# Three blocks in one program: first slabs k-tile by k-tile, the router in rounded parts, a norm factor applied later, and block 3's weights in rounded halves

## The reference, cut to what matters

```python
# block 1: rms_norm -> RWKV-7 heads and differential attention, each times a sigmoid gate, then an MLP
gates = jax.nn.sigmoid(p_gate).reshape(bsz, seqlen, N_BRANCH, D_MODEL)
merged = gates[:, :, 0] * o_rwkv + gates[:, :, 1] * o_diff
h_res = h_res + merged @ w_out[layer]
# block 2: layer_norm -> three linear-attention mixers -> branches -> ln1 -> 16 experts -> ln2
h = layer_norm(ALPHA * h + mix, ln1_g[l], ln1_b[l])
ffn = grouped_moe(h, w_router, router_bias, w_gate[l], w_up[l], w_down[l])
h = layer_norm(ALPHA * h + ffn, ln2_g[l], ln2_b[l])
# block 3: four attentions of four heads each on one projection, silu gates, one output projection
hn = rms_norm_3(x, norm_gain)
proj = jnp.einsum('btd,de->bte', hn, w_in)
...
return x + jnp.einsum('bte,ed->btd', y, w_out)
```

## Time and profile before

| what | us |
|---|---|
| median of 3 runs | 3912.48 (3900.85 to 3927.08) |
| the profiled execution's own time | 3914.93 |
| its span, first to last instruction | 3913.0 |
| PE busy | 3478.7 (89%) |
| weight loads busy | 2787.6 (71%) |
| DVE / ACT / POOL busy | 1604.3 / 1237.1 / 360.7 |
| mean granted clock of PE | 0.905 of full speed |

### The profile page before, as it was taken

The page is one execution under the profiler, slowest core; times in us unless marked ns, Lnnn a source line. Parts: engine busy times, 40 slices in busy tenths (PEclk is TensorE's granted clock), DMA queues, the critical chain, the costliest instruction groups (busy, mean ns, idle before and its releaser), DMA issues.

```text
span 3913.0 us, 69039 instructions
## 1 busy us (share of the span) xinstructions
PE 3478.7 (89%) x29806; PEld 2787.6 (71%) x29806; DVE 1604.3 (41%) x2836; ACT 1237.1 (32%) x2049; POOL 360.7 (9%) x337
## 2 busy tenths in 40 slices
PE   7888898889788999998788878879899999889998
PEld 6767777778668999996566666657578878355544
DVE  4443544454423343333445355566543344321222
ACT  3223322232322233233434455432222221232341
POOL 4121121112102100000011001110000000000000
PEclk9788897798859999999988889989899999988998
DMA  3001010011004233321112112123133333211111
GB/s 118 21 29 31 21 37 28 23 32 37 21 10 151 86 109 92 92 87 54 55 49 63 46 55 70 55 110 100 46 92 92 92 92 92 67 41 43 33 49 38
DMA packets 72448, 240.70 MB, mean 62 GB/s; under 512 B 8272, under 2 KB 8272, under 8 KB 70736
## 3 DMA queue, kind: packets, MB, share of 16 engines
q1 hardware_dynamic: 65088, 209.17, 17.8%
q0 software_dynamic: 3600, 20.83, 1.4%
q10 hardware_dynamic: 3456, 6.29, 0.4%
HBM read 221.44 MB, written 14.81 MB: 60 GB/s over the span
## 4 chain that ended last, share of the span: by engine, by line
PE 76%; DVE 11%; ACT 9%; issue 3%; DMA 1%; ACTq 0%; DVEq 0%; POOL 0%; SPq 0%; POOLq 0%
PE psum L410 74%; DVE arena L346 5%; ACT arena L331 5%; ACT arena L339 3%; DVE arena L355 2%; PE psum L414 1%; ACT L327 1%; DVE ring L346 1%; DVE arena L350 1%; ACT L331 1%; DMA ring<-in_w 1%; DVE arena L358 0%; DVE arena L367 0%; DVE arena L373 0%; DVE arena L370 0%
## 5 line engine op out<-in xcount | busy, mean ns | idle before, releaser
L410 PE MATMUL psum<-arena,ring 128*128 128x264 f32 (+2 forms) x6248 | 1576.7, 352 | 16.2 <-DVE arena L346 10.6
L410 PE MATMUL psum<-arena,arena 128*128 128x264 f32 (+2 forms) x6160 | 1498.4, 346 | 52.8 <-DVE ring L346 19.8
L410 PE MATMUL psum<-arena 32*32 32x32 f32 (+18 forms) x16376 | 1085.6, 248 | 319.8 <-ACT arena L331 82.4
L410 PEld LDWEIGHTS psum<-arena 32*32 32x32 f32 (+12 forms) x16376 | 771.2, 139 | 623.8 <-issue 277.6
L410 PEld LDWEIGHTS psum<-arena,arena 128*128 128x128 f32 (+1 forms) x6160 | 1013.2, 192 | 218.1 <-issue 52.9
L410 PEld LDWEIGHTS psum<-arena,ring 128*128 128x128 f32 (+1 forms) x6248 | 999.4, 197 | 208.3 <-issue 128.7
L339 ACT ACTIVATE arena<-psum 128x512 f32<-128x512 f32 (+12 forms) x625 | 282.8, 452 | 926.7 <-PE psum L410 817.6
L346 DVE TENSOR_TENSOR ring<-ring,arena 128x1024 fp32r<-128x1024 f32 (+1 forms) x297 | 354.3, 1193 | 515.2 <-ACT arena L339 511.2
L339 ACT ACTIVATE arena<-ring 128x1024 fp32r<-128x1024 f32 (+1 forms) x297 | 304.6, 1026 | 604.7 <-PE psum L410 552.3
L346 DVE TENSOR_TENSOR arena<-arena 128x528 f32<-128x528 f32 (+9 forms) x660 | 327.2, 496 | 245.3 <-ACT arena L331 130.4
L346 DVE TENSOR_TENSOR arena<-arena,psum 88x192 f32<-88x192 f32 (+5 forms) x428 | 193.5, 452 | 536.5 <-PE psum L410 526.2
(11 more groups left out here) (39 smaller groups left out, 840.3 us busy)
## 6 DMA issues: line engine op xcount, KB each, us to landing
ring<-in_w SPq DMA_DIRECT2D x313, 512.0 KB, 3.5
ring<-in_w SPq DMA_DIRECT2D x134, 256.0 KB, 2.6
bg<-arena ACTq DMA_DIRECT2D x24, 256.0 KB, 2.0
arena<-in_x SPq DMA_DIRECT2D x2, 2112.0 KB, 11.4
arena<-bg POOLq DMA_DIRECT2D x1, 3072.0 KB, 17.2
od<-arena POOLq DMA_DIRECT2D x8, 264.0 KB, 2.4
oy<-arena POOLq DMA_DIRECT2D x8, 264.0 KB, 2.4
arena<-oy POOLq DMA_DIRECT2D x2, 1056.0 KB, 7.8
```

The lines of the kernel that those rows point to most:

```text
L410: self.last_ins = self.eng.matmul(out, l, r, start=start, stop=stop, skip_group_check=skip)
```

## The change

- **Gates.** The gate products of k = 2 move to the heads' end, behind PE's `end` event, with their weight halves made by POOL before its oy transfer and their sigmoids on ACT ahead of the gates stage's first copies. Six buffers instead of four hold the gates. In block 1 ACT's root for kk comes one step earlier.
- **Mixers.** The first two slabs are computed together, k-tile by k-tile (`pe_two3`).
- **Branches.** The first four slabs (four high buffers instead of three) are split ahead of the waits for the mixers' ends. ln1's mean sum is spread over the last eight linears (`pe_add`), and the experts' first slabs are split before ln1.
- **Experts.** x's high part is made by ACT and the low part by DVE from the scaled value; slabs 0 and 1 follow k-tile by k-tile. The router comes behind them in three rounded products per k-tile with the router weights as the stationary side, is turned back by four transposes (`scores`), and DVE's router steps stand behind expert 0's products. The shares are turned behind slab 4. ln2's mean sum is spread as ln1's.
- **Block 3.** x's rounded parts times the gain are made without the norm's root; the sum of squares, the forget product and the first q product run together k by k. The root is multiplied in when DVE takes each product out of PSUM. All slabs come in halves that POOL splits, and all products are in rounded parts. v is computed like the others, then transposed. y is split for the last projection.

```diff
@@ -571,13 +571,19 @@
...
+    if run.highs >= len(run.offs) and run.then:
+        act_more(K, run.then)
+    else:
+        act_hi(K, run, run.highs)
+        run.highs += 1
...
@@ -594,6 +600,26 @@
...
+
+
+def pe_two3(K, first, second, xh, xl, of):
+
+    P, T, todo = K.P, xh[0].shape[1], []
+    for wh, wl, emptied, m in (first, second):
+        todo.append((wh, wl, K.ps[0:m, 512 * P.bank(1, *emptied):][:, 0:T], m))
+    for k in range(8):
+        P.wait_ge(*K.book.at(*of[k]))
+        for n, (wh, wl, out, m) in enumerate(todo):
+            P.mm3([out], wh(k)[:, 0:m], wl(k)[:, 0:m], xh[k], xl[k], k == 0, k == 7)
+            if k == 7:
+                yield n
+
+
+def pe_add(K, b, src, k, *of):
+
+    P, T = K.P, src.shape[1]
+    P.wait_ge(*K.book.at(*of))
+    P.mm(K.ps[:, 512 * b:512 * b + T], K.c["ones"], src, k == 0, k == 7)
...
@@ -1046,24 +1072,29 @@
...
+    for g in range(2):
+        gate(g, 2)
...
@@ -1088,7 +1119,7 @@
...
-                if nme == "v" and step == 1:
+                if nme == "v" and step == 0:
                     A.wait_ge(*at("rw_kk", hp))
                     A.inv_root(h2(m.dd[2]), out_of(K, 2, T, "rw_kkroot", hp), "rw_kkroot", hp, bias=K.c["tiny"])
...
@@ -1196,6 +1227,8 @@
...
     A.stage_end("act", "heads")
+    for g in range(2):
+        act_gate(K, m, g, 2)
...
@@ -1631,7 +1664,8 @@
...
-    assert m.wr.lows == len(m.wr.offs) or not K.book.known
+    while m.wr.lows < len(m.wr.offs):
+        pool_half(K, m.wr)
     G.wait_ge(*at("end", "pe", "heads"))
...
@@ -1957,7 +1991,8 @@
...
-               wh[0:3], [("slab", "mixers", 68)] * 3)
+               wh[1:4] + wh[0:1], [("slab", "mixers", 65 + i) for i in range(4)])
+    m.wx.then = m.wb
...
@@ -2053,13 +2089,10 @@
...
+    two = [pe_take(K, m.wx, w0)[1:] + (("gd_lr",), 40), pe_take(K, m.wx, w0 + SLAB)[1:] + (("gd_pad", 0, 0), 128)]
+    for i in pe_two3(K, *two, m.hh_r, m.h_r, [("normed", "ln0", k) for k in range(8)]):
+        P.did("slab", "mixers", i)
+        P.also(*(("gd_proj", 0, 0) if i else ("gd_lrp",)))
...
@@ -2839,34 +2876,44 @@
         pe_lin3(K, m.wb, i, ("b_y", i), m.Oh_r, m.O_r, [("b_Osplit", j) for j in range(12)], 4, 4 * (i % 3))
...
+        if k == 0:
+            b = K.P.bank(1, "centred", "ln1", 7)
+            K.P.keep(b)
+        else:
+            pe_add(K, b, m.h[:, (k - 1) * T2:k * T2], k - 1, "b_h", k - 1)
+    pe_add(K, b, m.h[:, 7 * T2:8 * T2], 7, "b_h", 7)
+    K.P.did("mean", "ln1")
+    K.P.drop(b)
...
     A, at, T = K.A, K.book.at, T2
+    act_first(K, m.wb)
     A.wait_ge(*at("end", "pe", "mixers"))
     A.wait_ge(*at("end", "dve", "mixers"))
     A.wait_ge(*at("end", "pool", "mixers"))
-    act_first(K, m.wb)
...
+    dve_first(K, m.wb)
+    split_dve(V, m.Oh_r[11][:], m.O[:, 11 * T:12 * T], m.O_r[11][:], "b_Osplit", 11)
     V.wait_ge(*at("end", "pe", "mixers"))
     V.wait_ge(*at("end", "act", "mixers"))
     V.wait_ge(*at("end", "pool", "mixers"))
-    dve_first(K, m.wb)
-    split_dve(V, m.Oh_r[11][:], m.O[:, 11 * T:12 * T], m.O_r[11][:], "b_Osplit", 11)
...
@@ -2891,9 +2938,12 @@
...
+        if k == 7:
+            dve_more(K, m.we)
+            dve_more(K, m.we)
...
@@ -2917,29 +2967,54 @@
...
+            P.mm3([ps[0:16, 512 * b:512 * b + 512]], m.wrh[:, R], m.wrl[:, R], m.xh_r[k], m.x_r[k], k == 0, k == 7)
...
+    def shares():
+        P.wait_ge(*at("r_w"))
+        b = P.bank(1, "r_ct")
+        for j in range(4):
+            P.tr(ps[0:16, 512 * b + 128 * j:512 * b + 128 * j + 128], m.R["w"][:, 16 * j:16 * j + 16])
+        P.did("r_tr")
+
+    two = [pe_weights(K, m.we, i) + (("e_up" if i else "e_silu", 0, 0), 128) for i in range(2)]
+    for i in pe_two3(K, *two, m.xh_r, m.x_r, [("e_xlow", j) for j in range(8)]):
+        P.did("slab", "experts", i)
+    router()
+    i = 2
...
-            for f in range(2):
...
+            for f in range(2) if e else (1,):
...
+                if e == 0:
+                    scores()
+                if e == 1 and f == 0:
+                    shares()
                 pe_lin3(K, m.we, i + 1, ("e_up", e, f), m.xh_r, m.x_r)
+                if e == 1 and f == 0:
+                    P.wait_ge(*at("r_ct"))
+                    share(0)
                 i += 2
-            if e == 0:
...
-                P.wait_ge(*at("r_ct"))
-            b = P.bank(1, "e_share", e)
-            P.mm(ps[:, 512 * b:512 * b + 512], s16[0:16, e, :], m.cT[0:16])
-            P.did("e_row", e)
+            if e:
+                share(e)
...
@@ -2950,19 +3025,25 @@
...
+    for k in range(8):
+        A.wait_ge(*at("ln1_g", k))
+        A.act(m.xh_r[k][:], m.x[:, k * T:k * T + T], ACT.Identity, "e_xhi", k, bias=K.p["ln1_b"][:, k:k + 1])
     A.wait_ge(*at("end", "pe", "branches"))
     A.wait_ge(*at("end", "dve", "branches"))
-    act_first(K, m.we)
...
@@ -2987,21 +3071,64 @@
...
+    dve_first(K, m.we)
+    V.wait_ge(*at("root", "ln1"))
+    for k in range(9):
+        if k < 8:
+            S = slice(k * T, k * T + T)
+            V.stt(m.x[:, S], m.h[:, S], p["ln1_g"][:, k:k + 1], m.rs, MUL, MUL, "ln1_g", k)
+        if k:
+            V.wait_ge(*at("e_xhi", k - 1))
+            V.stt(m.x_r[k - 1][:], m.x[:, (k - 1) * T:k * T], p["ln1_b"][:, k - 1:k], m.xh_r[k - 1][:], ADD, SUB, "e_xlow", k - 1)
     V.wait_ge(*at("end", "pe", "branches"))
     V.wait_ge(*at("end", "act", "branches"))
-    dve_first(K, m.we)
...
+            if e == 0:
+                dve_router(K, m, e3)
+                V.wait_ge(*at("r_tr"))
+                V.cp(m.cT[0:16], out_of(K, 1, T, "r_ct", m1=16), "r_ct")
+            V.wait_ge(*at("e_row", e))
+            for f in range(2):
+                kx = 2 * (e % 8) + f
+                S = slice(kx * T, (kx + 1) * T)
+                if e == 8 and f == 0:
+                    V.wait_ge(*at("slab", "experts", 47))
+                V.tt(m.Hl[:, S], m.esg[f], out_of(K, 1, T, "e_share", e), MUL, "e_sg", e, f)
+                if f:
+                    K.book.put(("e_share", e), K.book.now["e_sg", e, f])
+                split_dve(V, m.Hh_r[kx][:], m.Hl[:, S], m.Hl_r[kx][:], "e_H", half, kx)
...
@@ -3192,33 +3280,35 @@
...
+        for half in range(2):
+            wh, wl, over = pe_half(K, m.wz, off + half * HALF)
+            for k in range(4):
+                kx = 4 * half + k
+                P.mm3([bk(b)], wh(k), wl(k), m.hh_r[kx], m.h_r[kx], kx == 0, kx == 7)
+                if k == 1:
+                    yield
+            P.did(*over)
+            if half == 0:
                 yield
-        P.did(*done)
+        P.also(*done)
         P.drop(b)
 
...
+    def turned(t):
+        P.wait_ge(*at("fx_vt", t))
+        b = P.bank(1, "fx_v", t)
+        for J in J4:
+            P.tr(bk(b)[:, J], of_tile(m, t)[0].g[:, J])
+        P.did("fx_vtr", t)
...
@@ -3345,13 +3439,37 @@
...
+    b, bf, bq = P.bank(1, "root", "n3"), P.bank(1, "fx_forget"), P.bank(1, "fx_q", 0)
+    for half in range(2):
+        fh, fl, f_over = pe_half(K, m.wz, w0 + half * HALF)
+        qh, ql, q_over = pe_half(K, m.wz, w0 + SLAB + half * HALF)
+        for k in range(4):
+            kx = 4 * half + k
+            pe_add(K, b, m.y[:, kx * T:kx * T + T], kx, "sq", "n3", kx)
+            if kx == 7:
+                P.did("sum", "n3")
+            P.wait_ge(*at("fx_low", kx))
+            P.mm3([bk(bf)[0:4]], fh(k)[:, 0:4], fl(k)[:, 0:4], m.hh_r[kx], m.h_r[kx], kx == 0, kx == 7)
+            if k == 3:
+                P.did(*f_over)
+                P.also("fx_flin")
+            P.mm3([bk(bq)], qh(k), ql(k), m.hh_r[kx], m.h_r[kx], kx == 0, kx == 7)
+        P.did(*q_over)
+        P.also("fx_proj", 0, "q")
...
@@ -3494,15 +3622,27 @@
...
+        V.wait_ge(*at("fx_proj", t, n))
+        V.stt(x, bk("fx_" + n, t), 0.125 if n == "q" and not gain else 1.0, m.rs, MUL, MUL, "fx_" + n, t)
...
+    def v_tile(t):
         for _ in range(3):
             yield
+        V.wait_ge(*at("fx_proj", t, "v"))
+        V.tt(of_tile(m, t)[0].g, bk("fx_vt", t), m.rs, MUL, "fx_vt", t)
...
@@ -3533,8 +3673,18 @@
...
+        ready.append(t)
+
+    def splits():
+
+        for n in range(8):
+            while 5 not in ready or len(ready) <= n:
+                yield
+            t = ready[n]
+            split_dve(V, m.yh_r[t][:], m.y[:, t * T:t * T + T], m.y_r[t][:], "fx_ysplit", t)
+            yield
 
...
@@ -3606,16 +3758,32 @@
...
+    ready = []
+    V.wait_ge(*at("root", "ln2"))
+    for k in range(9):
+        if k < 8:
+            S = slice(k * T, k * T + T)
+            V.stt(m.centred[:, S], m.centred[:, S], p["ln2_g"][:, k:k + 1], m.scale, MUL, MUL)
+            V.ts(m.x[:, S], m.centred[:, S], p["ln2_b"][:, k:k + 1], None, ADD, None, "normed", "ln2", k)
+        if k:
+            V.wait_ge(*at("fx_hi", k - 1))
+            V.stt(m.h_r[k - 1][:], m.x[:, (k - 1) * T:k * T], p["ng3"][:, k - 1:k], m.hh_r[k - 1][:], MUL, SUB, "fx_low", k - 1)
...
@@ -3625,14 +3793,19 @@
...
+    for i, taken in enumerate(m.wz.after):
+        while m.wz.lows < taken + 3:
```

(4 more changed lines are left out.)

358 lines of the change are left out of this document (187 added, 171 removed).

## The result

| | before | after |
|---|---|---|
| median of 12 runs each, us | 3907.89 (3890.79 to 3927.08) | 3883.49 (3869.59 to 3893.8) |
| profiled execution, its own time | 3914.93 | 3869.59 |
| PE / DVE / ACT / POOL busy | 3478.7 / 1604.3 / 1237.1 / 360.7 | 3401.8 / 1642.8 / 1239.1 / 520.2 |

A forecast was written before the change was run, and what follows sets the result against it. PE was taken as the bound (72.0% of block 3's chain), with holes at stages' beginnings. The terms sum to -56.7; 3914.9 - 56.7 - 2 = 3856 us, range 3815 to 3893.

The forecast's parts named there:

- Gates: Gates' beginning: 12.0 us of gate work moves into PE's hole, first result 9.5 us later; -2.5 us (bounds -12, +2).
- kk root: Block 1's heads: ACT delivers kk's root one step sooner, so DVE waits less; -1 us (bounds -8, +8).
- Mixers: Mixers' first two slabs k-tile by k-tile: both results at about 1856, now 1852.3 and 1857.7; 0 us (bounds -3, +3).
- Branches' beginning: Start of branches: four slabs split before, so PE starts 4.6 us earlier, then waits for a ring slab; -2.8 us (0, -7).
- Mean sums: Mean sums spread over the last linears: only the last sum waits for DVE; +1.6 us in branches and experts (0, +4).
- Experts' beginning: Experts' start: earlier PE start, but waits behind slab 4 and ahead of slab 6; -3 us (bounds -20, +4).
- Block 3's beginning: From ln2's root: forget and q0 both done at 3387, so q0 comes for 0.8 us; -6 us (bounds 0, -13).
- Block 3's slabs: Block 3's 31 slabs in rounded halves: 41.3 us of PE saved, 36.4 on the chain, 4.4 back; -32 us (-12, -41).
- Last projection: End of block 3: 56.9 us for eight slabs become 8 x 5.55 + 1.5; -11 us (bounds -8, -12).
- rival 3: Block 3: POOL starves PE, about 4.4 us a half, so the kernel gets slower, 3963 us; chance 0.04.
- Rival 2: Block 3's saved PE time turns into waits: -12 instead of -32, -8 for the end, 3880 us; chance 0.20.
- rival 1: Whole kernel: covers hold everywhere, holes give what they show, block 3 loses nothing; -95, 3818 us; chance 0.15.

The follow-up runs named there:

- kk_as_before: The kernel after, with the root of kk back one step later in block 1; 3893.67 us, ratio 0.9959 to the kernel before.
- drop_late: The kernel after, with the mean's bank released behind the sum of squares at ln1 and ln2; 3875.13 us, ratio 0.99 to the kernel before.
- shares_late: The kernel after, with router-weight transposes and expert 0's share behind slab 5, and DVE's low part of slab 6 directly behind the router; 3873.39 us, ratio 0.9894.
- pool_short: The kernel after, with POOL's subtraction in block 3 cut to 8 of 512 columns and PE reading the weights' high part for the low; 3876.15 us, ratio 0.9907.
- forget_late: The kernel after, with DVE's forget gate steps eight rounds later, behind all tables' steps; 3885.45 us, ratio 0.9922 to the kernel before.
- factors_out: The kernel after, with the norm factor left out of block 3's q, k, v and g, which ACT copies from PSUM as before; 3878.15 us, ratio 0.991.

## Why the prediction was off

The sign was right, the gain less than half of the 57 us forecast. Two terms of the sum hold nearly all of the difference: block 3's slabs (23 us) and the mean sums (13 us). Step by step, by the pair of profiled executions:

- **Gates, -2.5 forecast, +0.3 measured** (190.7 to 191.0 us from the sigmoid of gate (1,1) to the MLP). The mechanism was right: the sigmoids stand ahead of the copies, and DVE turns to oy late. The first result comes 11.5 us later after the heads' end (30.8 against 19.4) where I had 9.5; the 2 us more are the third slab's DMA, which I had as landed.
- **kk root, -1**: not settled. The pair can't tell, and the medians of kk_as_before suggest some 10 us, more than my bounds of 8.
- **Mixers, 0**: counted from ln0's first high part, the first result is copied out 1.0 us later than before and the second 2.8 us earlier. What is left of that at the end can't be told (+0.3, in a stretch that varies by 9 us).
- **Branches' beginning, -2.8**: -3.2. But the wait for a ring slab came 22 us behind the first slab (2584.86 to 2607.1 us), not 17, after seven slabs where I had six, and it lasted 4.1 us instead of 2.2.
- **Mean sums, +1.6 (0 to +4)**: the clearest failure in kind, with +14.6 measured. At ln1 it cost 6.2 us, the mean steps between the slabs included. At ln2 it cost 3.2 us behind the last slab and 5.2 ahead of it: from the experts' slab 7 to their last matmul it takes 517.6 us (2803.87 to 3321.43), where it took 512.3 (2831.57 to 3343.88). I wrote that only the last sum has to wait for DVE; I didn't follow the bank that the spread sum holds. drop_late gives 12.4 us back and leaves 2.2, so in these executions the bank is the whole of the error: without it the term would have been right.
- **Experts' beginning, -3 (-20 to +4)**: -6.3, from a hole that looked like 20. Slab 7 starts 67.1 us behind ln1's root instead of 73.4; the -1.1 of the table has the 5.2 us of ln2's mean steps in it. The two holes forecast (6.4 us behind slab 4, and DVE's splits plus low part of 4.8 ahead of slab 6) measured 6.55 and 5.20. shares_late shows what the order cost: 10.5 us.
- **Block 3's beginning, -6**: PE starts on the tables 23.9 us behind the root with q0 done; before, the forget product was done 23.5 us behind it, and q0 was still to do. q0 (6.9 us) came for 0.4: -6.5.
- **Block 3's slabs, -32 (-12 to -41)**: the term that failed most in size. Start and end of the block give -15.8, less 6.5 for the beginning leaves -9.3, outside its bounds by 3 us. Three things explain nearly all of the 23 us: POOL's subtractions beside DVE's steps 14.0 us, which I had put at nothing in the sum; the DVE hop with the norm factor 4.4, which I had called even; the forget steps ahead of the tables 4.4; together 20.9 when taken out at once. The last one I had not seen at all: its queue order belonged in the working. The 5.55 us a slab of my working is a figure from stretches at the full clock; here the clock fell from 0.88 to 0.84, and PE's busy time by 28.7 us instead of 41.3.
- **Last projection, -11**: -10.3. DVE's step comes every 5.60 us, where I had 5.55.

The error in the collisions has one sentence: "as DVE is only some 5% of the chain, under 3 us of it would count". The price was about right: 15 us of DVE time forecast by an estimate, 11 us measured as busy time (161 to 150). But I weighted it by DVE's share of the chain before. The Trainium skill ("SBUF — State Buffer", section "SBUF: two separate sides") says that a DVE step with two inputs in SBUF and a POOL instruction that reads SBUF lock one port pair, and that the second of them blocks fully. The rows of pool_short agree, with 919 against 757 ns, and so does the PSUM form, which stayed at 692; in the round shown, the stretched 128x256 step ends 0.3 us behind POOL's subtraction. Shares of a chain hold for that kernel alone. When PE's part shrinks, the rounds in which DVE was just covered come onto the chain, and there a stretched DVE step counts: DVE's part of the chain fell by 12 us with the subtractions cut. The stretch gave 14 us for these, 5.4 as waits of PE and 7.6 as PE's busy time at the higher clock. POOL itself was never late: its halves took 0.64 + 1.29 us as forecast, so rival 3 did not come about, none of PE's waits over 0.1 us there is put down to POOL, and POOL has 2 us of the chain.

Rival 2 named the outcome, saved PE time that turns into waits (-12 and -8, 3880 us), and came within 4 us of it. That is partly luck: its reason, lost cover, is some 6 us of what the runs show, and its other parts left out the 13 us of the mean sums. That the time lies in my range owes something to luck too: the range was drawn around the rivals' middles, and the bank was in none of them. Two slips in the working change nothing here: 23 x 1.32 + 7 x 1.6 is 41.6 and not 41.3, for 30 slabs and not 31, and all better bounds together are -116, where rival 1 takes -95.

What stays open: some 2 of the 23 us in block 3, the place of the kk root, and what sets the granted clock behind a wait, in block 3's middle and at the norms' sums. With the three causes out PE's busy time was 9 us shorter at the higher clock, 8 of them already with POOL's subtractions alone; but forget_late alone had 6 us less and factors_out 2 us more, so no clean division comes out of these runs.
